# A hybrid S5 and sparse attention layer on one core: S5 states ahead of the second lag matrices, own scratch for the lag factors, key selection in earlier units

## What is computed

```python
# S5 group: 32 groups of 16 channels with 64 complex states each
bu = einsum('blgc,gpc->blgp', u, bb)            # per token and group
x  = associative_scan(x[l] = a * x[l-1] + bu[l])  # over the 512 tokens
y  = einsum('blgp,gcp->blgc', xr, c_re) - einsum('blgp,gcp->blgc', xi, c_im) + d_skip * u
y  = gelu(y);  y_ssm = y * sigmoid(y @ w_glu + b_glu)

# sparse attention group: 8 heads of 64; keys picked by an indexer
s_idx = sum over heads of relu(qi . ki) * wi    # causal
sel   = top_k(s_idx, 128)                       # 128 keys for each query
y_attn = softmax over sel of (q . k / 8)  times v
```

## Time and profile before

| | us |
|---|---|
| median of 3 runs | 779.82 (778.79 to 779.87) |
| profiled execution | 777.24 |
| its span, first to last instruction | 775.4 |
| TensorE busy | 710.9 |
| VectorE busy | 466.4 |
| ScalarE busy | 338.0 |
| GpSimd busy | 263.3 |

### The profile page before, as it was taken

How to read it: one execution, slowest core, us unless ns; L and a number is a source line. 1 busy time by engine, 2 the same in 40 slices (tenths; PEclk the granted TensorE clock), 3 DMA queues, 4 the chain that set the end, 5 groups by cost and what they waited for, 6 DMA issues and landing times.

```text
span 775.4 us, 9889 instructions
## 1 busy us (share of the span) xinstructions
PE 710.9 (92%) x3566; PEld 562.6 (73%) x3566; DVE 466.4 (60%) x818; ACT 338.0 (44%) x508; POOL 263.3 (34%) x209
## 2 busy tenths in 40 slices
PE   0798999998788879889799999999999999999997
PEld 0586876777574547678698888888878887888886
DVE  2868897976999787878653665764455455000005
ACT  4543356655422644432466455554544554111110
POOL 2003998239702200000022444344334434433440
PEclk9999999999879989899989999999999999999999
DMA  9951231260273633673811323322331332233202
GB/s 336 355 149 55 59 105 55 96 177 0 33 79 74 202 145 113 268 271 109 298 55 34 123 63 106 108 76 86 108 108 57 106 108 82 81 109 108 84 26 108
DMA packets 63080, 91.46 MB, mean 118 GB/s; under 512 B 12010, under 2 KB 41474, under 8 KB 62979
## 3 DMA queue, kind: packets, MB, share of 16 engines
q1 hardware_dynamic: 59520, 89.44, 36.3%
q10 hardware_dynamic: 3523, 1.54, 0.7%
HBM read 86.28 MB, written 4.69 MB: 117 GB/s over the span
## 4 chain that ended last, share of the span: by engine, by line
PE 76%; DVE 15%; ACT 4%; issue 3%; DMA 1%; SPq 0%; ACTq 0%; DVEq 0%
PE bank L1574 23%; PE bank L1575 22%; PE bank L1576 22%; PE bank L1579 2%; DVE arena L1123 2%; DVE arena L1283 1%; PE bank L1921 1%; DVE stat L1280 1%; PE bank L1809 1%; DVE w_lo L1133 1%; DMA xh<-in_x 1%; DVE stat L1072 1%; DVE arena L1147 1%; PE bank L1916 1%; PE bank L1789 1%
## 5 line engine op out<-in xcount | busy, mean ns | idle before, releaser
L484 POOL TENSOR_TENSOR w_lo<-w_raw,w_hi 128x2048 fp32r<-128x2048 f32 x34 | 156.8, 4612 | 390.7 <-ACT w_hi L678 192.5
L1574 PE MATMUL bank<-act_hi,w_hi 128*128 128x512 f32 (+2 forms) x384 | 148.1, 386 | 4.8 <-DVE act_lo L1511 3.2
L1575 PE MATMUL bank<-act_lo,w_hi 128*128 128x512 f32 (+2 forms) x384 | 146.9, 383 | 0.0
L1576 PE MATMUL bank<-act_hi,w_lo 128*128 128x512 f32 (+2 forms) x384 | 146.8, 382 | 0.0
L1574 PE MATMUL bank<-w_hi,act_hi 128*128 128x512 f32 x240 | 100.9, 420 | 4.2 <-ACT arena L744 3.1
L1575 PE MATMUL bank<-w_lo,act_hi 128*128 128x512 f32 x240 | 96.7, 403 | 0.0
L1576 PE MATMUL bank<-w_hi,act_lo 128*128 128x512 f32 x240 | 96.6, 403 | 0.0
L678 ACT ACTIVATE w_hi<-w_raw 128x2048 fp32r<-128x2048 f32 x26 | 49.7, 1912 | 89.9 <-PE bank L1576 87.1
L1574 PEld LDWEIGHTS bank<-act_hi,w_hi 128*128 128x128 f32 x384 | 73.2, 191 | 19.7 <-issue 3.9
L1575 PEld LDWEIGHTS bank<-act_lo,w_hi 128*128 128x128 f32 x384 | 73.2, 191 | 14.3 <-issue 0.2
L1576 PEld LDWEIGHTS bank<-act_hi,w_lo 128*128 128x128 f32 x384 | 73.2, 191 | 14.3
(11 more groups left out here) (305 smaller groups left out, 1182.2 us busy)
## 6 DMA issues: line engine op xcount, KB each, us to landing
w_raw<-in_w_up SPq DMA_DIRECT2D x44, 512.0 KB, 4.6
arena<-in_w_ada SPq DMA_DIRECT2D x16, 1024.0 KB, 10.8
w_raw<-in_w_down SPq DMA_DIRECT2D x22, 512.0 KB, 3.9
w_raw<-in_w_in SPq DMA_DIRECT2D x10, 1024.0 KB, 5.1
xh<-in_x SPq DMA_DIRECT2D x8, 512.0 KB, 7.8
w_raw<-in_w_out SPq DMA_DIRECT2D x4, 1024.0 KB, 12.2
s_mem<-in_w_ada SPq DMA_DIRECT2D x4, 1024.0 KB, 7.0
arena<-in_w_ada SPq DMA_DIRECT2D x2, 2048.0 KB, 10.8
```

The costliest lines, as they stand in the source:

```text
L484: nc.gpsimd.tensor_tensor(w_lo[:, slot, 0:width], w_raw[:, slot, 0:width], w_hi[:, slot, 0:width].bitcast(F32), ALU.subtract).then_inc(S[" ...
L1574: T.matmul(dst, lhs_hi, rhs_hi, start=start, stop=False)
L1575: T.matmul(dst, lhs_hi, rhs_lo, start=False, stop=False)
L1576: return T.matmul(dst, lhs_lo, rhs_hi, start=False, stop=stop)
```

## The change

The stage `states` of half 0 moves from unit 11 to unit 8, `u` of half 1 from 12 to 9, `states` of half 1 from 13 to 10, and `lags` of half 1 from 10 to 12. The waits of TensorE are changed with the order of use of banks 6 and 7. `weigh_lags` gets a scratch of its own, `lag_part`, which lies where tile 0 and 1 of the attention output (`y_attn`) come later; so ScalarE's copy of `u` for half 1 into `up32` waits on the second source of V (`vt_ready`) in place of the second lag factors, and VectorE's first `heads_out` waits on those (`lag_w_ready`). The 16 rounds of each tile's key selection are spread anew: three rounds for tile 1 ahead of the loop and 13 in units 0 to 3 (before: 16 in units 0 to 7), those of tile 2 in units 4 to 11 (before: 8 to 11), those of tile 3 in units 12 to 22 (before: 16 to 23).

```diff
-         6: ("u", 0, 0), 7: ("lags", 0, 0), 10: ("lags", 1, 0), 11: ("states", 0, 0), 12: ("u", 1, 0), 13: ("states", 1, 0),
+         6: ("u", 0, 0), 7: ("lags", 0, 0), 8: ("states", 0, 0), 9: ("u", 1, 0), 10: ("states", 1, 0), 12: ("lags", 1, 0),
...
-ROUNDS = {**{i: 2 for i in (*range(8), *range(16, 24))}, **{i: 4 for i in range(8, 12)}}
+ROUNDS_AHEAD = 3
+ROUNDS = {1: {0: 2, 1: 2, 2: 4, 3: 5}, 2: {4: 2, 5: 2, 6: 2, 7: 2, 8: 2, 9: 3, 11: 3},
+          3: {12: 1, 13: 2, 14: 2, 15: 2, 16: 2, 17: 2, 18: 1, 19: 1, 20: 1, 21: 1, 22: 1}}
...
-    t = i // HEADS + 1
-    return ((t,),) * ROUNDS.get(i, 0), ((t,) if i < 24 and i % HEADS == 7 else ())
+    return tuple((t,) for t in ROUNDS for _ in range(ROUNDS[t].get(i, 0))), (
+        (i // HEADS + 1,) if i < 24 and i % HEADS == 7 else ())
...
+        lag_part = cut(6144, 1024)
...
-                t1 = up32[:].rearrange("p a n -> p (a n)").rearrange("p (g l h) -> p g l h", g=GH, l=CHUNK)
+                t1 = lag_part.rearrange("p (g l h) -> p g l h", g=GH, l=CHUNK)
...
                         if half and i == 0:
-                            act.wait_ge(S["lag_w_ready"], 2)
+                            act.wait_ge(S["vt_ready"], 2)
...
                 dve.wait_ge(S["pv_done"], HEADS * (t + 1))
+                if t == 0:
+                    dve.wait_ge(S["lag_w_ready"], 2)
...
+            top_k(((1,),) * ROUNDS_AHEAD, ())
             ada_at = [0]
             for i in range(0, ATT_UNITS, 2):
...
                     if half == 0:
-                        pe.wait_ge(S["lags_ready"], 4)
+                        pe.wait_ge(S["lags_ready"], 2)
...
-                    pe.wait_ge(*((S["u_t_read"], 2), (S["lags_ready"], 2))[half])
+                    pe.wait_ge(*((S["u_t_read"], 2), (S["state_read"], 2))[half])
...
                     else:
-                        pe.wait_ge(S["state_read"], 2)
+                        pe.wait_ge(S["lags_ready"], 4)
```

## The result

| | before | changed |
|---|---|---|
| median of 5 runs each, same chip | 778.79 us (777.4 to 779.87) | 786.83 us (783.87 to 790.87) |
| changed / before | | 1.0101, 95% interval 1.0067 to 1.0136 |
| profiled execution, its span | 777.24, 775.4 us | 790.87, 789.1 us |
| granted clock, mean of the span | 0.969 | 0.955 |

The changed kernel is slower by 8.0 us at the medians; the forecast was +3.0, with 782.8 in place of 786.83. The sign and the way to y(0) held, the size was short by five. 786.83 lies just inside the stated range of 778.3 to 787.

A forecast was written before the change was run, and what follows sets the result against it. VectorE was read as the engine waited for up to 234.75 us, then a serial ScalarE and TensorE chain from y(0). Terms: +9.3 - 3.16 - 3.14 = +3.0 us, so 782.8 against the median shown; range 778.3 to 787.

The forecast's parts named there:

- The start of y(0): First S5 product of half 0 on TensorE: to start at 247.5 us instead of 238.19, 9.3 us later.
- Rival (d): VectorE was the bound, so its 10.7 us lead reaches y(0): -6.3 us, 773.5; chance 0.15.
- The wait of 2.4 us ahead of the first addition: VectorE, before adding D to lags(0): a new 2.4 us wait for ScalarE's second copy of the lags.
- The wait ahead of the second: VectorE, before adding D to lags(1): a 2.6 us wait for ScalarE's copy, which ends at 243.9.
- GpSimd's hold: GpSimd's two subtractions, about 235.9 to 245.0, may hold VectorE's addition to lags(1), which then ends at 245.3.
- Down to the end: From y(0) through the glu products: +9.3 - 3.16 - 3.14 = +3.0 us, the shift then going to the end.
- The idle 3.16 us: TensorE's idle stretch before the first glu product: to vanish, since one VectorE round is left at unit 22; -3.16 us.
- The product: First glu product on TensorE: to take 3.93 us instead of 7.07 with no idle stretch ahead, 3.14 us less.
- The rigid part: y(0) to the transposes of g: moves as a block, no step waiting on VectorE beyond a few tenths; y(1) 13.07 behind.
- Rival (a): The lower clock stays at the first glu product, costing 3.14 us: +6.1, 785.9; chance 0.15.
- Rival (b): Full TensorE clock in the middle, lags(1) in 3.65 us: -0.2, 779.6, or +1.6, 781.4 if GpSimd holds the addition; chance 0.22.
- Rival (c): Eight loads for y(1) land late, past a 3.3 us cover: at twice the time +8, 790; chance 0.05.

The follow-up runs named there:

- E11: The changed kernel run again as it is, for a second profile; ratio 1.0107 to the kernel before, 787.19 us.
- E1: Changed kernel with the S5 stages and TensorE's waits back in the old order, new rounds and scratch kept; ratio 0.9987 to the kernel before, 776.88 us.
- E6: Changed kernel with the three tile 3 rounds of units 12 and 13 moved to units 16 to 18; ratio 1.0085 to the kernel before, 788.14 us.
- E4: Changed kernel with one filler matmul ahead of the transposes of units 15, 17 and 21; ratio 1.0068 to the kernel before, 784.56 us.
- E3: Changed kernel with lags(1) at unit 11 instead of 12 and GpSimd's two subtractions behind the additions; ratio 1.0076 to the kernel before, 784.78 us.
- E8: Kernel before with only the lag factors' own scratch and its two waits; ratio 1.0008 to the kernel before.
- E2: Changed kernel with the selection rounds spread as before, S5 order and scratch as changed; ratio 1.0258 to the kernel before, 798.69 us.
- E7: Kernel before with the two rounds of unit 22 moved to units 16 and 17; ratio 0.9969 to the kernel before, 781.13 us.
- E9: E5 with GpSimd's two subtractions waiting for product y(1); ratio 0.9930 to the kernel before, 774.81 us.
- E5: E1 with no tile 3 round before unit 15, its 16 rounds in units 15 to 21; ratio 0.9889 to the kernel before, 774.83 us.
- E10: E9 with filler matmuls ahead of logits 14, y(0) and the transposes of units 15, 17 and 21; ratio 0.9883 to the kernel before, 769.63 us.
- E12: E7 with filler matmuls ahead of logits 12, y(0) and the transposes of units 15, 17 and 21; ratio 0.9911 to the kernel before, 771.38 us.

## Why the prediction was right in sign and short in size

**The start of y(0): right.** Forecast 9.3 us late; 9.1 and 9.3 (E11) against before's profile, 9.9 if the two profiles each of the old order (39.15 and 37.72) and of the changed one are averaged. Without the 2.9 us that lie ahead, y(0) starts at 247.3, inside the forecast 246 to 248. TensorE was to stand idle from 226 to 236; it did from 230.1 to 239.4, which is 227.2 to 236.5 without the 2.9. E1 shows that the order is the cause, and E6 that the rounds aren't. Rival (d), VectorE as the bound, is out: its lead reached scan 1 and was lost behind it, at the place that the prediction names.

**The pieces of that way: mostly right, two waits off.** The three rounds ahead of unit 0 fitted: 0.24 us of the 2.95 us wait are left. The wait before unit 4 was filled as well; the nine rounds ended at 190.36, 14.1 us behind the first logits, where VectorE waited up to 15.0 us behind them before (E11 has 0.96 us of the 5.80 left). The wait of 2.4 us ahead of the first addition isn't there in the changed kernel's profile (E11 has 0.65), since VectorE came later to it. The wait ahead of the second was 0.98 us and not 2.6: the prediction let both of its additions wait for the second copy of ScalarE, while the first needs only the first copy, which came at 244.45, 1.75 us ahead of the second. Neither lies on the way to y(0).

**GpSimd's hold: right, and without effect.** The additions for half 1 took 3.30 us, 3.44 in E11, 3.47 in E6 and 3.56 in E4 while GpSimd was at its subtractions, and 0.35 in E3 where it waited. That is the rule which the prediction cited from the Trainium skill, SBUF — State Buffer, "Who interferes with whom", and the traces agree by these numbers. As the prediction said, TensorE's own path is no shorter: logits 16 follow the fillers at 249.10 with no wait.

**Down to the end: the step that failed.** "y(0) to the transposes of g goes rigidly", and behind it "with no idle stretch ahead of it I take 3.93", made -6.3. By the profiles it is less. The old order took 51.19 and 54.01 us from y(0) to the second glu product (before, E8), the changed one 50.71 and 47.85 (changed, E11); the means differ by 3.3. With y(0) 9.9 us late on the mean, the second glu product is 6.6 us late, and 8.0 were measured at the end. The profiles have the 1.4 left behind the glu stage, which the prediction took as the same work: from the second glu product to the end it is 488.25 and 488.02 us for the changed kernel and 486.02 and 486.40 for the old order, 1.9 more on the mean, and 8.5 from lags(0) to the end. The order of issue doesn't bring that by itself, since E6 took 485.83. Two profiles of each are few. Three parts of the term can be told apart:

- The idle 3.16 us went, as said, in every kernel with no round left ahead of the first glu product.
- The product came down as sized wherever the clock rose: from first to second glu product 4.94 to 4.98 us, forecast 4.97, in 9 of the 11 profiles with no wait ahead (the others 7.47 and 8.15), and 7.38 to 8.11 in three of three with it. So the term holds, most of the time; in the profile that opened this section it is 0.64 instead of 3.14.
- The rigid part wasn't rigid: this is the term that was mis-sized. y(0) to y(1) took 14.70 and 15.13 us and not 13.07, y(1) to glu 28.54 and 27.77, where before's busy part had 26.85. Its granted clock was 0.86 to 0.89. One profile of the kernel before had been drawn at 1.00, and the prediction took it for the kernel's. With fillers (E4) the stretches are 13.07, 26.62 and 4.98, and y(0) to the second glu product is 44.67 against 51.19, the forecast's 6.3 within 0.2.

What lowers the clock in one execution and not in another stays open. The order of issue alone doesn't. From y(1) to the first glu product the new order shows 0.86, 0.89 and, with the old rounds (E2), 0.88, but 1.00 in E6 and in E3 (lags(1) a unit earlier); the old order shows 1.00 in two profiles and 0.86 in E7, and E1's order 1.00 in E1 and E9 and 0.85 in E5. So the changed kernel's two profiles don't show that it runs at a lower clock than the one before.

**Rival (a)**, the low clock staying at the first glu product, is what the first profile shows and what E11 doesn't. The low clock came at another place than the prediction put it: in the middle. In that first profile the product took 6.43 us, close to the 7 us that the prediction had named as a sign of being wrong; in E11 it is down.

**Rival (b)**, the full clock in the middle, is out: ahead of y(0) the states product took 3.39 us and lags(1) 5.23, both near the times that the prediction took. **Rival (c)**, late loads, is out too: the eight loads were issued from 250.94 to 254.68 and landed 5.9 us after issue by the median, some 260.6 for the last, and y(1) started at 264.84 with no wait ahead of it.

**The number itself** was in part luck. +8.0 lies outside the +0.5 to +5 that the forecast gave itself, and is nearest to the +6.1 of rival (a). It is inside the stated range, by 0.2 us, because that range was drawn around the rivals too.

## What to carry to other kernels

When a product is moved ahead or back, follow everything that stands between it and the next engine's release, on every queue it shares: filling early waits pays only if what stands ahead of the next awaited product gets shorter. Here the same early rounds were worth nothing (E1), more than half of a loss (changed, against E2) or 1.1% (E5), by what was put ahead of scan 1. And a sum down to 3 us in 780 should not take the duration of a stretch from one execution where TensorE has short waits in it: look for the lowest and the highest clock at which that kind of stretch has run, or fill the waits with matmuls first.

## What the runs showed of the hardware that was not expected

- Around short waits TensorE's clock was lower in one execution and not in another, with the same 114 matmuls in the same order: 13.07 us at 1.00 (before) and 15.92 at 0.79 (E8). With fillers in the waits the stretch took 13.07, 13.07 and 13.08 (E4, E10, E12); without them 14.60 to 17.59 in ten of eleven profiles.
- A small VectorE instruction was held for 3.3 to 3.6 us beside GpSimd's long subtractions, a tensor_scalar with one tensor input among them (3.62 against 0.36); yet taking the hold away gave nothing that 12 runs could show (E9).
- The kernel before ran from 772 to 790 us over all comparisons, on several chips, so that a profile's own total says little about 1%.
